# MLP down phases: evacuation by ScalarE copies and accumulating DMAs in place of VectorE

## What is computed

```
h = rms_norm(x, norm_mlp_g[l])
x = x + jnp.square(jax.nn.relu(h @ w_mlp_up[l])) @ w_mlp_down[l]
```

## Time and profile before

| | |
|---|---|
| median of 3 runs | 2650.54 us (2650.3 to 2650.7) |
| the profiled execution | 2650.98 us |
| its span, first to last instruction | 2649.3 us |
| PE matmul busy | 2640.2 us, 100% |
| PE weight loads busy | 2233.5 us, 84% |
| DVE busy | 1986.9 us, 75% |
| ACT busy | 1366.9 us, 52% |
| GpSimd busy | 30.3 us, 1% |
| DMA | 511.06 MB, mean 193 GB/s |

### The profile page before, as it was taken

One profiled execution on the slowest core, in us unless ns is written; L12 is line 12 of the kernel. 1 busy time (PEld: TensorE's weight loads), 2 busy tenths in 40 slices (PEclk: granted clock), 3 DMA queues, 4 the chain that ended last, 5 costly groups with the idle time before them and its releaser, 6 DMA issues.

```text
span 2649.3 us, 39598 instructions
## 1 busy us (share of the span) xinstructions
PE 2640.2 (100%) x13478; PEld 2233.5 (84%) x13478; DVE 1986.9 (75%) x2876; ACT 1366.9 (52%) x1865; POOL 30.3 (1%) x64
## 2 busy tenths in 40 slices
PE   9999999999999999999999999999999999999999
PEld 7888888888888888888888888888788888888887
DVE  6687876555555778798797567878787978879886
ACT  6455555444444554555554454456555555455453
POOL 0100000000000000000000000000000000000000
PEclk9999999999999999999999999999999999999999
DMA  7655556665655566556566555545555655655565
GB/s 277 236 175 182 190 173 197 204 201 194 203 191 188 177 199 205 187 196 198 190 206 210 190 176 175 173 150 191 171 175 190 199 198 192 205 190 196 187 205 175
DMA packets 141721, 511.06 MB, mean 193 GB/s; under 512 B 16134, under 2 KB 16439, under 8 KB 141464
## 3 DMA queue, kind: packets, MB, share of 16 engines
q1 hardware_dynamic: 136312, 493.86, 55.9%
q0 software_dynamic: 3840, 12.86, 1.5%
q10 hardware_dynamic: 1440, 2.62, 0.3%
HBM read 505.08 MB, written 4.21 MB: 192 GB/s over the span
## 4 chain that ended last, share of the span: by engine, by line
PE 96%; DVE 2%; ACT 1%; DMA 0%; issue 0%; SPq 0%; ACTq 0%; DVEq 0%
PE acc L1955 26%; PE acc L1952 13%; PE acc L1973 5%; PE acc L1991 4%; PE acc L1993 4%; PE acc L1992 4%; PE pS L1991 3%; PE pS L1993 3%; PE pT L1993 3%; PE pT L1991 3%; PE pS L1992 3%; PE pT L1992 3%; PE acc L1970 2%; PE pO L1991 2%; PE pO L1993 2%; PE pG L1993 2%
## 5 line engine op out<-in xcount | busy, mean ns | idle before, releaser
L1104 DVE TENSOR_TENSOR wlo<-raw,whi 128x1024 fp32r<-128x1024 f32 x938 | 1143.4, 1223 | 446.4 <-ACT whi L614 440.5
L614 ACT ACTIVATE whi<-raw 128x1024 fp32r<-128x1024 f32 x938 | 990.0, 1057 | 793.7 <-PE pT L1993 243.1
L1955 PE MATMUL acc<-a_w,whi 128*128 128x512 f32 x2944 | 935.8, 397 | 0.1
L1952 PEld LDWEIGHTS acc<-a_w,wlo 128*128 128x128 f32 x2944 | 553.2, 188 | 129.4
L1952 PE MATMUL acc<-a_w,wlo 128*128 128x256 f32 x2944 | 578.6, 278 | 0.0
L1955 PEld LDWEIGHTS acc<-a_w,whi 128*128 128x128 f32 x2944 | 451.5, 189 | 2.5 <-DVE a_w L1157 0.8
L1973 PE MATMUL acc<-a_w,whi 128*128 128x512 f32 x592 | 198.4, 404 | 0.0
L825 ACT ACTIVATE t<-acc 128x256 f32<-128x256 f32 x128 | 48.9, 382 | 170.0 <-PE acc L1955 169.9
L1970 PEld LDWEIGHTS acc<-a_w,wlo 128*128 128x128 f32 x592 | 111.4, 188 | 24.5
L1970 PE MATMUL acc<-a_w,wlo 128*128 128x256 f32 x592 | 116.8, 279 | 0.0
L1500 DVE TENSOR_TENSOR t<-acc,t 128x256 f32<-128x256 f32 x128 | 54.0, 422 | 74.9 <-ACT t L825 74.8
(11 more groups left out here) (496 smaller groups left out, 3962.8 us busy)
## 6 DMA issues: line engine op xcount, KB each, us to landing
raw<-stream SPq DMA_DIRECT2D x938, 512.0 KB, 3.4
gbias<-gateb POOLq DMA_DIRECT2D x12, 256.0 KB, 4.1
X<-x_rows POOLq DMA_DIRECT2D x4, 512.0 KB, 6.8
bias_scratch<-brow POOLq DMA_DIRECT2D x8, 256.0 KB, 5.5
q<-bias_scratch POOLq DMA_DIRECT2D x8, 256.0 KB, 3.8
out<-X ACTq DMA_DIRECT2D x8, 256.0 KB, 5.3
xF<-x SPq DMA_DIRECT2D x6, 256.0 KB, 6.8
bias<-bias_scratch POOLq DMA_DIRECT2D x8, 128.0 KB, 4.1
```

What stands on the lines that cost most here:

```text
L614: A(whi[:, slot, :], raw[:, slot, :], ACT.Copy).then_inc(s.hi_done, 1)
L1104: TT(wlo[:, slot, :], raw[:, slot, :], whi[:, slot, :].bitcast(F32), SUB).then_inc(s.lo_done, 1)
L1952: low = lambda: MM(ps[:, 0:T], wl, wide[:, k0 + k, 0:T], start=False, stop=False, skip_group_check=True)
L1955: last = MM(ps, wh, wide[:, k0 + k, :], start=start and k == 0, stop=not start and k == KC - 1, skip_group_check=True)
```

## The change

ACT takes over the evacuation of the two-phase groups. It copies each bank into one of six SBUF buffers (drain), columns with the factor rsq, parts without; GpSimd waits for the copy and issues a DMA that adds the buffer to X or to the part in SBUF (accum_op=add). Per layer there are DRAINS = 40 such adds: 8 in group 0 (its parts are copied by ACT straight into the part tiles), 16 in group 1 and 16 in group 2. ACT waits before a copy until the add that used the same buffer six copies earlier has landed. In phase 0 the four columns stand at the same places as DVE's did; the four parts of phase 0 follow at t = 0 of phase 1 in place of 1 and 2; the rest stays at its places. GpSimd's 40 adds of layer 0 stand ahead of its wait for the added parts, those of layer 1 at its end. DVE waits at the second tile of a layer's last group until all adds have landed. PE waits for m_free as before, which ACT now gives. WARM goes from 5 to 8, and the DMA scratch in SBUF is set to 4096 bytes.

The core of the diff:

```
-WARM = 5
+WARM = 8
+NDRAIN = 6
+DRAINS = 8 + 16 + 16
...
+        def drains_landed(eng, layer):
+
+            for k in range(NDRAIN):
+                eng.wait_ge(drain_added[k], 16 * len(range(k, DRAINS * (layer + 1), NDRAIN)))
...
+            def add(dst):
+
+                k = added[0]
+                added[0] += 1
+                pool.dma_start(dst, drain[:, k % NDRAIN, :], accum_op=ALU.add).then_inc(drain_added[k % NDRAIN], 16)
+
+            def add_columns(i, n):
+
+                for h in range(2):
+                    pool.wait_ge(s.t_evac, 2 * (i + n) + h + 1)
+                    add(X[:, h, COLS * n:COLS * n + COLS])
+
+            def add_parts(layer, g, q):
+
+                for n in range(4):
+                    pool.wait_ge(s.m_free, 4 * phase(layer, g, q) + n + 1)
+                    add(parts[q][n])
+
+            def add_drains(layer, i0):
+
+                for g in range(FF_GROUPS - 1):
+                    i = i0 + 4 * g
+                    add_columns(i, 0)
+                    add_columns(i, 1)
+                    if g:
+                        add_parts(layer, g, 0)
+                        add_parts(layer, g, 1)
+                    add_columns(i, 2)
+                    add_columns(i, 3)
+
+            add_drains(0, G_MLP1)
             pool.wait_ge(s.m_added, 8)
...
+            add_drains(1, G_MLP2)
...
+            def drain_bank(ps, scale, freed):
+
+                k = drained[0]
+                drained[0] += 1
+                if k >= NDRAIN:
+                    act.wait_ge(drain_added[k % NDRAIN], 16 * (k // NDRAIN))
+                A(drain[:, k % NDRAIN, :], ps, ACT.Copy, scale=scale).then_inc(freed, 1)
+
+            def drain_parts(layer, g, q, banks):
+
+                act.wait_ge(s.block_done, BLOCK_CHUNKS_AFTER[phase(layer, g, q)])
+                if layer and not g:
+                    act.wait_ge(s.m_added, 8)
+                for n in banks:
+                    ps = (acc[0], acc[1], pV, pN)[n]
+                    if g:
+                        drain_bank(ps, 1.0, s.m_free)
+                    else:
+                        A(parts[q][n], ps, ACT.Copy).then_inc(s.m_free, 1)
...
+                        for t in range(16):
+                            if q and t == 0:
+                                drain_parts(layer, g, 0, (0, 1, 2, 3))
+                            if q and t in (12, 13):
+                                drain_parts(layer, g, 1, (0, 1) if t == 12 else (2, 3))
+                            if q and t >= 14:
+                                act.wait_ge(s.t_half, i + t - 13)
+                                column(t - 14, 0)
+                                act.wait_ge(s.mm_done, c + t + 1)
+                                column(t - 14, 1)
+                            if not q and t == 14:
+                                act.wait_ge(s.rb_ready, 4 if layer else 2)
+                                act.wait_ge(s.t_evac, 2 * i)
+                                act.wait_ge(s.t_half, i + 1)
+                                column(0, 0)
+                            if not q and t == 15:
+                                act.wait_ge(s.block_corner, p + 1)
+                                column(0, 1)
+                                act.wait_ge(s.t_half, i + 2)
+                                column(1, 0)
+                                column(1, 1)
+                            prep(At(c + t))
...
-                            if q and t in (1, 2):
-                                part_sums(layer, g, 0, (0, 1) if t == 1 else (2, 3))
-                            if q and t in (12, 13):
-                                part_sums(layer, g, 1, (0, 1) if t == 12 else (2, 3))
...
+                        if ends and m == 1:
+                            drains_landed(dve, layer)
+                            dve.wait_ge(s.t_evac, done)
...
-    nc = bacc.Bacc("TRN2", target_bir_lowering=False, num_devices=1)
+    nc = bacc.Bacc("TRN2", target_bir_lowering=False, num_devices=1, dynamic_dma_scratch_size=4096)
```

More of the change, by code:

```diff
@@ L362, in program @@
         tsm = sb("tsm", 48)[0]
+        drain = sb("drain", NDRAIN * COLS)[0].rearrange("p (k c) -> p k c", k=NDRAIN)
         ssq = tsm[:, 0:16].rearrange("p (s h n) -> p s h n", s=2, h=2)
@@ L478, in program @@
         wg_landed = [ctx.enter_context(nc.semaphore(f"wg_landed{k}")) for k in range(2)]
+        drain_added = [ctx.enter_context(nc.semaphore(f"drain_added{k}")) for k in range(NDRAIN)]
         gb_landed = [ctx.enter_context(nc.semaphore(f"gb_landed{k}")) for k in range(2)]
@@ L574, in _ @@
                     pool.dma_start(gbias[n % 2], gateb[:, D * g + COLS * q:D * g + COLS * q + COLS]).then_inc(gb_landed[n % 2], 16)
+            added = [0]
+            def add(dst):
[21 more added lines that the diff above has]
+            add_drains(0, G_MLP1)
             pool.wait_ge(s.m_added, 8)
@@ L807, in _ @@
                             mix_hi(At(3))
+            drained = [0]
+            def drain_bank(ps, scale, freed):
[14 more added lines that the diff above has]
+                        A(parts[q][n], ps, ACT.Copy).then_inc(s.m_free, 1)
             def mlp(b, a, i0, layer, stage, gain, before):
@@ L833, in up, with down_pair, column @@
                             A(mixed_hi[:, m.base // 2, :], mixed, ACT.Copy).then_inc(s.mixed_hi, 1)
+                    def down_pair(q):
+                        c, i = b + 64 * g + 32 + 16 * q, i0 + 4 * g + 2 * q
+                        def column(e, h):
+                            drain_bank(tbanks(At(i + e), True)[h], rsq[:, h:h + 1], s.t_evac)
+                        for t in range(16):
[20 more added lines that the diff above has]
+                            prep(At(c + t))
                     def down(n, last):
@@ L860, in mlp @@
                         up(At(15))
-                    for n in range(NG):
-                        down(n, g == FF_GROUPS - 1)
+                    if (layer, g) in SECOND_GROUPS:
+                        down_pair(0)
+                        down_pair(1)
+                    else:
+                        for n in range(NG):
+                            down(n, g == FF_GROUPS - 1)
             mlp(B_MLP1, A_MLP1, G_MLP1, 0, 1, "g_mlp1", G_OUT1 + NG - 1)
@@ L1449, in part_sums @@
                     dve.wait_ge(s.block_done, BLOCK_CHUNKS_AFTER[r])
[L1450 to L1453, removed]
+                    dve.wait_ge(s.m_free, 4 * r)
                 for n in banks:
                     ps, part = (acc[0], acc[1], pV, pN)[n], parts[q][n]
[L1456 to L1459, removed]
+                    TT(part, ps, part, ADD).then_inc(s.m_free, 1)
             def part_mix(layer, q, f):
@@ L1521, in down_pair @@
                         for t in range(16):
-                            if q and t in (1, 2):
-                                part_sums(layer, g, 0, (0, 1) if t == 1 else (2, 3))
-                            if q and t in (12, 13):
-                                part_sums(layer, g, 1, (0, 1) if t == 12 else (2, 3))
[L1526 to L1532, removed]
+                            if (layer, g) not in SECOND_GROUPS and t == 14:
                                 dve.wait_ge(s.t_half, i + 1)
                                 corner(0, 0)
-                            if not q and t == 15:
+                            if (layer, g) not in SECOND_GROUPS and t == 15:
                                 dve.wait_ge(s.block_corner, p + 1)
```

## The result

The changed kernel takes 2671.38 us (median; 2669.98 to 2672.72), the kernel before on the same chip 2650.57 us: a ratio of 1.0078, 95% interval 1.0065 to 1.0091. The forecast was 2648.7 us, and 2671.4 lies above the upper end of the range, 2666.3. The profiled execution took 2670.91 us, 19.9 us more than that of before.

A forecast was written before the change was run, and what follows sets the result against it. TensorE was taken as the bound, busy 2640.2 of 2649.3 us; -1.9 us for six stalls and +0.1 us for zero products gave -1.8 us, so 2648.7 us from a median of 2650.54; range 2647.0 to 2666.3 us.

The forecast's parts named there:

- The six stalls of 0.32 us: PE's first product into acc of six second phases waits for DVE's part sums; removing this gains 1.9 us.
- the sum: Whole kernel: -1.9 us for the stalls and +0.1 us for zero products give -1.8 us.
- ACT's copies: 96 bank copies on ACT, 0.69 us with factor, 0.58 without, 61 us together; cost nothing if none waits for a buffer.
- the traffic: Down phase: sixteen 256 KB adds in 86.5 us, DMA share 0.62, about half the capacity free; weight-load delay costs nothing.
- The landing of an add: 256 KB accumulating DMA: 4.9 us from issue to landing, median plain load 4.1 plus one more read 0.8.
- the slower rival: Layer ends: adds at shared-engine pace, 4.3 us each, land 8.8 us late twice; 17.6 us, 2666.3 us; late adds 0.27.
- The wait for buffers: Four seams: eighth copy waits for the second add; free at 4.9 us landing, 15 us in all at 12.0.
- the slack of 4.2 us: Seam between a group's phases: DVE finishes the chunk at 1183.0, PE wants it at 1187.19.
- the second burst of a group: Four part copies, four columns: seventh copy comes 9 us after the first; slack larger than at the seam.
- the forecast's 1412.3: Layer end: PE's start on the last group's ninth chunk; its low half ends at 1408.3, leaving 4.0 us.
- Zero products: Launch: three more zero products delay the first real product by 0.1 us; upper bound 2.0 us.
- GpSimd's queue: 80 issues of 0.54 us in an otherwise empty queue keep up with copies every 0.6 us or slower; cost nothing.

## Why the prediction was wrong

**The gain was right.** The six stalls of 0.32 us are gone in the changed kernel, and with the adds' bytes taken away it runs at 2649.25 us, 1.4 us under the kernel before, where the sum had 1.8. The interval of that ratio just reaches 1, but all its runs (2648.37 to 2649.90) lie under those of before (2650.31 and up). What the change was worth without its transfers is near the forecast.

**ACT's copies were right.** Forecast 0.58 and 0.69 us; measured 0.59 to 0.60 (acc, pV, pN) and 0.68 to 0.69 (pO, pG, pS, pT). They hide where no add is late.

**The step that failed is the traffic**: "Weight loads are asked for several microseconds ahead of use, and I cost their delay at nothing". I read a mean share of 0.62 over 86.5 us and called half of the capacity free. But the adds don't come over 86.5 us. Eight of them are issued in 11 us, and with the 1.43 us that one takes, they are 11.4 us of all 16 engines, of which 1.6 us had been had by 1180 (27.2% of 6 us). In the 14 us from 1180 to 1194 the stream took 0.53 and 0.56 of the engines before, 7.6 us. That is 17.4 us of work for 14 us, in which the shares measured, 1.10 and 1.07, make 15.2. The windows of the kernel before and of the changed one (columns as in the earlier trace rows):

```profile
1180.00:1187.00 7.00, 7.00 (x33) 5.79 (x32) 6.96 (x9) 3.85 (x4) 0.00 (x0) 1.00 0.53 174
1187.00:1194.00 7.00, 6.96 (x31) 5.41 (x30) 6.93 (x9) 3.06 (x3) 0.00 (x0) 1.00 0.56 198
```

```profile
1180.00:1187.00 7.00, 7.00 (x33) 5.79 (x32) 4.48 (x7) 4.61 (x6) 1.81 (x3) 1.00 1.10 241
1187.00:1194.00 7.00, 7.00 (x33) 5.79 (x32) 4.00 (x3) 1.87 (x2) 0.00 (x0) 1.00 1.07 283
```

The prediction did name what would show it (whi waiting for raw), but gave it no price and no rival. The cover was not counted either: a tile that comes 5.6 us late (8.9 instead of 3.3) delays the sums of its pair, and those delay two conversions, for which three chunks of lead are too few.

**The landing of an add was sized for an add alone.** I took 4.9 us from issue to landing. One at a time that is what it was, 5.1 us in the median; in the bursts of the changed kernel it was 10.0, and the first burst's first add took 6.8 us from its issue at 1173.64 to the copy that it released at 1180.46. The rows of the adds, for the changed kernel and then for one add at a time:

```profile
DMA to landing us min/median/max: 5.7/10.0/14.4
```

```profile
DMA to landing us min/median/max: 3.2/5.1/7.4
```

The engine time was not sized too small where it was sized: the slower rival took two reads, 1.62 us, and 1.43 were measured. The sum on traffic just didn't use it. The rule of the Trainium skill that the prediction weighed (Collectives: The Full Stack, section "The bandwidth ceiling": a reduce reads two sources, so it has about half a copy's rate) is borne out here: 1.43 against 0.66 us is a factor of 2.2. By it the slower rival would have been the forecast.

**The wait for buffers came, and was survived.** ACT's timeline, which answers to the earlier trace rows:

```profile
1177.37 1.10 ACT L860 ACTIVATE drain<-acc 128x512 f32<-128x512 f32 x2
1180.46 0.60 ACT L860 ACTIVATE drain<-pV 128x512 f32<-128x512 f32 x1 [1.99 <-DMA X<-drain]
1182.99 0.60 ACT L860 ACTIVATE drain<-pN 128x512 f32<-128x512 f32 x1 [1.93 <-DMA X<-drain]
1183.49 2.00 ACT L657 ACTIVATE whi<-raw 128x1024 fp32r<-128x1024 f32 x2
...
1194.89 1.06 ACT L657 ACTIVATE whi<-raw 128x1024 fp32r<-128x1024 f32 x1 [5.76 <-DMA raw<-stream]
```

The second add lands 7.3 us after its issue, within the 8.2 us that the forecast allowed. The seventh and the eighth copy wait, not the eighth alone, and the conversion behind them comes at 1183.5, 2.8 us after the forecast's 1180.7. PE has its chunk at 1187 all the same: the slack of 4.2 us held. But slots are freed later, so the next loads start later, into the middle of the burst: the load of the chain above at 1185.97, with eight buffers at 1183.42. Eight buffers give back 5.9 us. In the second burst of a group, which the forecast held to be slack, six copies wait as well, 2.0 us at most.

**The slower rival had the shared engines and nearly the size, at the wrong place.** It let the adds run at the pace of shared engines (4.3 us each) and priced the end of the layer, 2666.3 us. The place is real, as the run with one add at a time shows (25.4 us of waiting, just there), and the changed kernel comes close to it. The last add of layer 0 lands at 1417.2, and VectorE stands still before its part mixing until then:

```profile
1417.50 0.69 DVE L1558 TENSOR_TENSOR part<-part,part 128x512 f32<-128x512 f32 x1 [2.61 <-issue]
```

The low half behind it ends at 1421.5. PE loses nothing by that, since it is itself 10.4 us later here than in the kernel before: the forecast's 1412.3 for this chunk becomes about 1422.7. The weight stream had paid first. The loss is 20.8 us, where the rival had 15.8.

**Zero products, scratch and GpSimd's queue** cost nothing that can be measured, as forecast, though an issue takes 0.86 us and not the 0.54 us of a plain load.

Left open: how the engines share out their time between the adds and the loads. The shares above say that the adds got 86.7% where the stream got 23.8%, but not how much the stream had asked for in that moment.

## What to carry to other kernels

Work given to DMA is priced in the stretch in which it comes, not by the mean share of a phase: add its engine time (here 1.43 us for an add of 256 KB, 0.66 for a plain write) to what the stream takes in the same microseconds, and set the sum against the lead of the next load. Where only a bank has to come free, a copy into SBUF by an engine with room does it without any transfer, and here the version that does so was 22.8 us faster than the one with adds. Pacing transfers so that they leave the stream alone moves the price to whoever waits for the last of them.

## What the runs showed that was not expected

After the stall of 3.67 us, the next products start 0.43 us apart instead of 0.227. The windows of the changed kernel give the granted clock, 0.98 and then 0.78 of full speed:

```profile
1194.00:1201.00 7.00, 3.50 (x15) 2.67 (x14) 4.29 (x6) 2.62 (x3) 0.00 (x0) 0.98 0.32 128
1201.00:1208.00 7.00, 6.32 (x22) 4.75 (x22) 6.51 (x8) 3.09 (x4) 0.00 (x0) 0.78 0.48 150
```

At the lower of TensorE's two levels, 1.2 GHz, eight products lost some 0.2 us each: 1.7 us on top of the stall. After the other stalls of this execution, 0.8 to 2.5 us, nothing of the kind is seen; with eight buffers it follows one of 2.29 us, with the larger scratch ones of 2.06 to 2.55. So a wait of a few microseconds can cost nearly half as much again, and its length alone doesn't say whether it will.

The launch shows it too, and with it what the three zero products may buy. In the profile of the run with earlier part sums, which has five, PE idles 2.06 us before the first real product at 9.51 us, and products then start 0.43 us apart until 13.13, at a granted clock of 0.64 and 0.61 (windows from 9.5 to 11 and to 14 us): 1.6 us. In the kernel before it idles 1.76 us there and loses nothing, with eight zero products alone 0.33. The medians of this case show no gain from it.
